# Hybrid decoder block: projection by quarters, the gates' log made in projection, and the experts' gate in one silu

## The reference

```python
hn = rms(x); proj = hn @ w_in              # 1024 -> s5 512 | q 512 | k 512 | v 512 | o 512 | gates 8
y1 = s5_mixer(u)                           # diagonal state space model, glu
q, k = silu(causal_conv(q, k))             # 4 taps
i_pre, f_pre = gates + bias                # 4 heads each
lf = log_sigmoid(f_pre)
y2 = mlstm(q, k, v, i_pre, lf)             # chunks, C, n and m carried; norm; * sigmoid(o)
h = x + concat(y1, y2) @ w_out
t = rms(h); top 4 of 32 experts, softmax gate
# each expert:
h1 = t @ w_up + b_up; g = min(h1[:, :1024], 7); lin = clip(h1[:, 1024:], -7, 7)
y = (g * sigmoid(1.702 * g) * (lin + 1)) @ w_down + b_down
out = rms(h + sum(gate * y))
```

## Time and profile before

| what | us |
|---|---|
| median of 3 runs | 2365.64 (2362.5 to 2370.26) |
| the profiled execution | 2366.74 |
| its span, first to last instruction | 2364.9 |
| project | 0 to 291 |
| mlstm | 294 to 395 |
| s5, output projection and router | 396 to about 655 |
| experts, first to last matmul | 660.5 to 2327 |

### The profile page before, as it was taken

The page is one execution under the profiler, slowest core; times in us unless marked ns, Lnnn a source line. Parts: engine busy times, 40 slices in busy tenths (PEclk is TensorE's granted clock), DMA queues, the critical chain, the costliest instruction groups (busy, mean ns, idle before and its releaser), DMA issues. The chain is left out here.

```text
span 2364.9 us, 32336 instructions
## 1 busy us (share of the span) xinstructions
PE 2166.7 (92%) x10370; PEld 1793.7 (76%) x10371; DVE 1696.4 (72%) x1961; ACT 1214.3 (51%) x1241; POOL 539.6 (23%) x538
## 2 busy tenths in 40 slices
PE   5999866889489999999999999999999999999993
PEld 4787866668368887887888878887887888878772
DVE  4688766646785665778679785887975798677774
ACT  3423143233164554657557664766754576565653
POOL 1001111102520111214124121422411242121411
PEclk9999976999689999999999999999999999999997
DMA  6123271541395666879779885988986798687964
GB/s 174 55 81 134 77 130 36 176 165 54 126 378 204 220 226 190 272 258 325 277 254 375 304 290 209 310 312 275 359 317 191 242 368 311 220 275 257 315 226 178
DMA packets 285814, 540.83 MB, mean 229 GB/s; under 512 B 37155, under 2 KB 53587, under 8 KB 284659
## 3 DMA queue, kind: packets, MB, share of 16 engines
q1 hardware_dynamic: 260306, 490.51, 60.0%
q0 software_dynamic: 25440, 49.47, 8.1%
HBM read 513.06 MB, written 64.57 MB: 244 GB/s over the span
## 5 line engine op out<-in xcount | busy, mean ns | idle before, releaser
L2369 DVE TENSOR_TENSOR ex_w_lo<-ex_raw,ex_w_hi 128x2048 fp32r<-128x2048 f32 x408 | 928.9, 2288 | 264.4 <-ACT ex_w_hi L2263 197.6
L2263 ACT CAST ex_w_hi<-ex_raw 128x2048 fp32r<-128x2048 f32 x371 | 708.2, 1912 | 255.3 <-PE ex_ps_l L2583 80.8
L2174 POOL TENSOR_TENSOR ex_passed<-ex_ident 128x1 f32<-128x1 f32 x136 | 105.2, 774 | 1215.6 <-ACT ex_y L2305 1195.5
L2582 PE MATMUL ex_ps_g<-ex_w_hi,ex_x_hi 128*128 128x512 f32 x784 | 309.2, 394 | 16.3 <-issue 6.4
L2582 PE MATMUL ex_ps_l<-ex_w_hi,ex_x_hi 128*128 128x512 f32 x784 | 308.9, 394 | 1.5 <-DVE ex_w_lo L2369 1.5
L2583 PE MATMUL ex_ps_g<-ex_w_lo,ex_x_hi 128*128 128x512 f32 x784 | 306.6, 391 | 0.0
L2583 PE MATMUL ex_ps_l<-ex_w_lo,ex_x_hi 128*128 128x512 f32 x784 | 305.4, 389 | 0.0
L2582 PE MATMUL ex_ps_y<-ex_w_hi,ex_h_hi 128*128 128x512 f32 x544 | 217.5, 400 | 6.8 <-DVE ex_h_lo L2405 6.8
L2586 PE MATMUL ex_ps_g<-ex_w_hi,ex_x_lo 128*128 128x512 f32 x544 | 212.7, 391 | 0.0
L2586 PE MATMUL ex_ps_l<-ex_w_hi,ex_x_lo 128*128 128x512 f32 x544 | 212.1, 390 | 0.0
L2583 PE MATMUL ex_ps_y<-ex_w_lo,ex_h_hi 128*128 128x512 f32 x544 | 212.0, 390 | 0.0
(11 more groups left out here) (459 smaller groups left out, 3770.9 us busy)
## 6 DMA issues: line engine op xcount, KB each, us to landing
ex_raw<-in_w_up_dram SPq DMA_DIRECT2D x272, 1024.0 KB, 8.2
ex_raw<-in_w_down_dram SPq DMA_DIRECT2D x136, 1024.0 KB, 8.2
st_tab<-tabs SPq DMA_DIRECT2D x8, 1408.0 KB, 7.8
pr_raw<-in_w_in_dram SPq DMA_DIRECT2D x10, 1024.0 KB, 5.5
tabs<-pr_x POOLq DMA_DIRECT2D x32, 256.0 KB, 2.3
por_raw<-in_w_out_dram SPq DMA_DIRECT2D x16, 256.0 KB, 4.4
t<-mix_sig_o SPq DMA_DIRECT2D x8, 512.0 KB, 2.6
fi_h<-h SPq DMA_DIRECT2D x8, 512.0 KB, 7.7
```

Of the source, the lines that this page charges most:

```text
L2174: pool.tensor_tensor(passed[:, :], ident[:, 0:1], ident[:, 0:1], ALU.add).then_inc(passed_done, 1)
L2263: nc.scalar.copy(w_hi[:, j % SPLIT, :, :], raw[:, j % RAW, :, :]).then_inc(hi_done, 1)
L2369: v.tensor_tensor(w_lo[:, j % SPLIT, :, :], raw[:, j % RAW, :, :], w_hi[:, j % SPLIT, :, :].bitcast(F32), ALU.subtract).then_inc(lo_done, 1)
L2582: pe.matmul(to[:, :], hi_in[:, b, kk, :], w_hi[:, s, k, :], start=first, stop=False)
```

## The change

In `project` SP loads tile 3 ahead of piece 1. TensorE turns tiles 0 and 1 and does units 0 to 3 on the first 256 tokens, then on the next 256, into the two halves of the same banks, with the turns of tiles 2 to 7 between. ScalarE and VectorE split piece 0 after tile 1 and piece 1 after tile 2, and put `turned_in` ahead of `square`, and `h_lo` ahead of `mean`. Abs, Exp and Ln of the gates come after the read of unit 40, and VectorE's `min - log` at the end of the block, in place.

In `mlstm` POOL does the memset of `toep` and makes `q_inter` of the next chunk ahead of `power`; VectorE does `gated` ahead of `scales`.

In `experts` ScalarE makes silu(1.702 g) instead of the sigmoid, so VectorE's multiply goes; the limit of the product is 1.702 times as high, and the factor is taken out when `hidden` is copied and split. TensorE does chunks 0 and 1 of the first block, then of the second. The semaphore `sig_done` goes and `glu_done` counts for both; the counts at the other waits are adapted (left out below).

```diff
+        f_abs = raw[0:HEADS, 0, 0:T // PC, :].rearrange("h k n -> h (k n)")
...
-                    if 1 <= j < 1 + PRAW:
-                        load_piece(sp, j - 1)
+                    if j in (1, 3):
+                        load_piece(sp, j // 2)
...
+                    turned_in(j)
+                    if j == 1:
+                        hi(0)
                     if j + 2 < TT:
                         square(j + 2)
-                    turned_in(j)
-                    if j in (1, 2):
-                        hi(j - 1)
+                    if j == 2:
+                        hi(1)
...
+                    if m == LOG_AT:
+                        act.wait_ge(lo_done, len(pieces))
+                        act.wait_ge(unit_read, read_count("gates", 0, 1))
+                        nc.scalar.activation(f_abs, mix["gates"][:, 1, :], ACT.Abs).then_inc(abs_set, 1)
+                        act.wait_ge(abs_set, 1)
+                        nc.scalar.activation(f_abs, f_abs, ACT.Exp, scale=-1.0).then_inc(exp_set, 1)
+                        act.wait_ge(exp_set, 1)
+                        nc.scalar.activation(f_abs, f_abs, ACT.Ln, bias=1.0).then_inc(log_set, 1)
...
-                for j in range(FIRST):
-                    turn(j)
+                turn(0)
+                turn(1)
+                for quarter in range(2):
+
+                    for m in range(FIRST):
+                        n, _, i, _ = units[m]
+                        if m == 0:
+                            pe.wait_ge(t_free, 2 * 2 * (quarter + 1))
+                        if quarter == 0 and i % TILES == 0:
+                            pe.wait_ge(lo_done, n + 1)
+                        cols = slice((i % TILES) * P, (i % TILES + 1) * P)
+                        toks = slice(quarter * 256, (quarter + 1) * 256)
+                        to = acc[m][:, toks]
+                        for k in range(KD):
+                            pe.matmul(to, w_hi[:, n, k, cols], h_hi[:, k, toks], start=(k == 0), stop=False)
+                            pe.matmul(to, w_hi[:, n, k, cols], h_lo[:, k, toks], start=False, stop=False)
+                            mm = pe.matmul(to, w_lo[:, n, k, cols], h_hi[:, k, toks], start=False, stop=(k == KD - 1))
+                        if quarter:
+                            mm.then_inc(unit_ready, 1)
+                            turn(FIRST + m)
+                        elif m < 2:
+                            turn(2 + m)
...
-                    if m < FIRST:
-                        turn(FIRST + m)
...
-                        mean(j + 2)
                     for half in range(2):
                         v.wait_ge(t_hi, 2 * j + half + 1)
                         v.tensor_tensor(h_lo[:, 4 * half:4 * half + 4, j * P:(j + 1) * P],
                                         ps_t[half][:, :].rearrange("p (k t) -> p k t", k=4),
                                         h_hi[:, 4 * half:4 * half + 4, j * P:(j + 1) * P].bitcast(F32),
                                         ALU.subtract).then_inc(t_free, 1)
-                    if j in (1, 2):
-                        lo(j - 1)
+                    if j == 1:
+                        lo(0)
+                    if j + 2 < TT:
+                        mean(j + 2)
+                    if j == 2:
+                        lo(1)
...
+                gate_f = mix["gates"][:, 1, :]
+                v.wait_ge(log_set, 1)
+                v.scalar_tensor_tensor(gate_f, gate_f, 0.0, f_abs, ALU.min, ALU.subtract).then_inc(log_f_set, 1)
+                v.wait_ge(log_f_set, 1)
...
+                pool.memset(st["toep"][:, :, :], 0.0).then_inc(st["zeroed"], 1)
+
+                def query(c):
                     pool.wait_ge(inter_done, c + 1)
                     if c >= 2:
 
                         pool.wait_ge(out_ready, c - 1)
                     pool.tensor_tensor(q_inter[:, c % 2, :, :], q[:, :, steps(c)], w_inter[:, :, :], ALU.mult).then_inc(q_done, 1)
+
+                query(0)
+                for c in range(NC):
+                    if c + 1 < NC:
+                        query(c + 1)
...
-                v.memset(st["toep"][:, :, :], 0.0).then_inc(st["zeroed"], 1)
-                gate_i, gate_f = mix["gates"][:, 0, :], mix["gates"][:, 1, :]
-                v.wait_ge(log_set, 1)
-                link(v.scalar_tensor_tensor(log_f[:, :], gate_f, 0.0, f_abs[:, :], ALU.min, ALU.subtract))
+                gate_i, log_f = mix["gates"][:, 0, :], mix["gates"][:, 1, :]
                 v.wait_ge(consts_set, 11)
-                link(v.tensor_tensor_scan(b[:, :], not_first[:, :], log_f[:, :], 0.0, ALU.mult, ALU.add))
+                link(v.tensor_tensor_scan(b[:, :], not_first[:, :], log_f, 0.0, ALU.mult, ALU.add))
...
+                        gated(c - LAG)
                     if c in NORM_AT:
                         scales(NORM_AT.index(c))
-                    if c >= LAG:
-                        gated(c - LAG)
...
-                        nc.scalar.copy(h_hi[:, b, 4 * half:4 * half + 4, 0:rows],
-                                       ps_t[i % 2][:, :].rearrange("p (k t) -> p k t", k=4)[:, :, 0:rows]).then_inc(
+                        nc.scalar.activation(h_hi[:, b, 4 * half:4 * half + 4, 0:rows],
+                                             ps_t[i % 2][:, :].rearrange("p (k t) -> p k t", k=4)[:, :, 0:rows],
+                                             ACT.Copy, scale=1.0 / ALPHA).then_inc(
...
-                def sigmoid(n, half, blocks, small):
+                def silu(n, half, blocks, small):
                     act.wait_ge(chunk_used, n * CHUNKS + (USED + 4 * half + 2))
                     if half:
                         act.wait_ge(hidden_done, n * 4 + 1)
                     for b in range(blocks):
                         if small and b:
-                            act.wait_ge(glu_done, n * 4 + (2 * half + 1))
+                            act.wait_ge(glu_done, n * 10 + (4 * half + 2))
                         ins = nc.scalar.activation(glu[:, row(half, b, blocks), :], g_bank(half, b, blocks)[:, :],
-                                                   ACT.Sigmoid, scale=ALPHA)
-                    ins.then_inc(sig_done, 1 if small else 2 + 4 * half)
+                                                   ACT.Silu, scale=ALPHA)
+                    ins.then_inc(glu_done, 1 if small else 4 + 2 * half)
...
-                        v.tensor_tensor(h_lo[:, b, rows, :], ps_t[i % 2][:, :].rearrange("p (k t) -> p k t", k=4),
-                                        h_hi[:, b, rows, :].bitcast(F32), ALU.subtract).then_inc(
+                        v.scalar_tensor_tensor(h_lo[:, b, rows, :], ps_t[i % 2][:, :].rearrange("p (k t) -> p k t", k=4), 1.0 / ALPHA,
+                                        h_hi[:, b, rows, :].bitcast(F32), ALU.mult, ALU.subtract).then_inc(
...
-                def gate(n, half, blocks, small):
-                    if small:
-                        fold(n, g_bank(half, 1, blocks), 0, 3 * half + 1).then_inc(glu_done, 1)
-                    v.wait_ge(sig_done, n * 8 + (3 * half + 2))
-                    for b in range(blocks):
-                        at = row(half, b, blocks)
-                        ins = v.tensor_tensor(glu[:, at, :], g_bank(half, b, blocks)[:, :], glu[:, at, :], ALU.mult)
-                    ins.then_inc(glu_done, 1 if small else 2)
+                def gate_fold(n, half, blocks):
+                    fold(n, g_bank(half, 1, blocks), 0, 4 * half + 1).then_inc(glu_done, 1)
...
-                        ins = v.scalar_tensor_tensor(hidden[:, at, :], glu[:, at, :], GLU_MOST, lin[:, at, :], ALU.min, ALU.mult)
+                        ins = v.scalar_tensor_tensor(hidden[:, at, :], glu[:, at, :], ALPHA * GLU_MOST, lin[:, at, :], ALU.min, ALU.mult)
...
-                def multiply(n, kind, j, blocks, full):
+                def multiply(n, kind, j, blocks, full, mine):
...
+                    for b in mine:
...
-                    mm.then_inc(chunk_used, 1)
+                    if mine[-1] == blocks - 1:
+                        mm.then_inc(chunk_used, 1)
 
                 def item(n, kind, blocks, full=None):
-                    for j in range(CHUNKS):
-                        multiply(n, kind, j, blocks, full)
+                    if blocks == 2:
+
+                        for b in range(2):
+                            for j in range(2):
+                                multiply(n, kind, j, blocks, full, (b,))
+                    for j in range(2 * (blocks - 1), CHUNKS):
+                        multiply(n, kind, j, blocks, full, range(blocks))
```

More of the change, by code:

```diff
@@ L2322, in item @@
                         if j in (1, 5):
-                            sigmoid(n, j // 4, blocks, small)
+                            silu(n, j // 4, blocks, small)
                         if j in (6, 8):
@@ L2336, in _ @@
                 act.wait_ge(bias_plus, 1)
-                nc.scalar.activation(warm[0:2 * E, :], bias_rows[0:2 * E, 0:1], ACT.Sigmoid).then_inc(y_a_read, 1)
```

(5 more changed lines are left out.)

43 lines of the change are left out of this document (18 added, 25 removed).

## The result

The changed kernel takes **2332.84 us** (median of 4 runs, 2331.74 to 2334.58), against 2364.07 for the kernel before beside it: the ratio is 0.9864, 95% interval 0.9844 to 0.9885, so it is faster by 31.2 us.

What follows compares the result with a forecast made beforehand. TensorE, busy 92% of the span, was taken as the bound, only its waits recoverable. Projection's start -5, log and mLSTM 0, experts -14.5 made -19.5 on 2364.9; forecast 2346 us, range 2336 to 2353 (8 in 10: 2334 to 2357).

Steps and rivals of the forecast that it cites:

- Projection's start: Projection up to unit 4: first matmul 10.8 us earlier, gain at unit 4 of 5 us, bounds 3 to 8.
- the clock rival: Projection's start: TensorE's clock halves after the new 2.1 us wait, losing 2 to 4 us (2349); no chance given.
- half speed at the start: Projection's first 4.1 us of matmuls run at half speed, costing 2 us before and after alike.
- Gates' log: Projection's end to mLSTM's first scan: log activations cost +1.2 us at projection's end, the scan gains -3.0 (2 to 4).
- mLSTM loop: mLSTM batches: query ahead of power delays the power 0.95 us, `gated` even at the second batch; cost +1.8 (0 to 3).
- The sign named for it: mLSTM's first batch: TensorE's wait for `k_state` would show 0.9 us longer.
- Experts, chunk order: Two-block experts: all four TensorE waits for `x_lo` or `x_hi` covered, -7.9 us (5 to 8.5).
- Experts, silu: Five one-block experts after a small pair: multiplies leave the path to `h_lo`, -6.0 us (0 to 14); `lin` waits stay.
- The half microsecond for refills: Experts: half a microsecond for refills of TensorE's pipe, counted into their total gain.
- its first rival: One-block experts: VectorE is the bound, so the 64 us taken from it come back as time; 2334, chance 0.1.
- the experts' sum of -14.5: Experts' total: chunk order -7.9, silu -6.0 and half a microsecond for refills.

Runs made afterwards that it cites:

- e2: The kernel before with only the gates' logarithm made in the projection and the `toep` memset on GpSimd: 2364.16 us, ratio 0.999.
- e12: The kernel before with only mLSTM's two orders (query ahead of the power, gated output ahead of the scales): 2369.32 us, ratio 0.998.
- e14: The kernel before with only VectorE's gated output put ahead of the scales in mLSTM: 2365.4 us, one run.
- e13: The kernel before with only GpSimd's query put ahead of the power in mLSTM: 2367.56 us, one run.
- e3: The kernel before with only the experts' new chunk order: 2352.5 us, ratio 0.9948.
- e1: The kernel before with only the projection's part (256-token quarters, loads and splits reordered; no log there): 2357.59 us, ratio 0.9965.
- e4: The kernel before with only the experts' silu (no gate multiply on VectorE), old chunk order: 2358.74 us, ratio 0.9972.
- e8: The changed kernel with one-block experts' second transposition of hidden rows issued inside chunk 9, after its first three matmuls: 2324.86 us, ratio 0.9832.
- e7: The changed kernel with 72 idle 128x128 transposes on TensorE ahead of mLSTM's first real one: 2334.21 us.
- e10: e8's kernel with 8 idle 512-column matmuls ahead of mLSTM and three more ahead of the state matmuls of chunks 3 and 5: 2326.53 us, ratio 0.9803.
- e11: The kernel before with 96 idle 4x4 transposes on TensorE at mLSTM's start: 2367.23 us, one run.

## Why the prediction was wrong

- **Projection's start**, -5 forecast, -5.8 measured. All marks held within 0.3 us up to the wait of 2.1 us; the clock rival is real and takes some 2 us in three profiles of nine. On average the term was right. What the prediction calls half speed at the start is the spacing of the matmuls, 0.41 us for 0.227; the granted clock of that row reads 1.00, and the cause of the spacing is open.
- **Gates' log**, +1.2 and -3.0 forecast, +0.3 and -4.05 measured; e2 alone had -3.1 for the second. The activations hide under the last unit's matmuls better than I had them, and GpSimd's constants started 2.8 us behind the last read's end instead of 3.8; why is open. The load shows no drain here either, 282.30 to 283.60.
- **mLSTM loop**, +1.8 forecast. This step failed in its sign: it is -1.8 (79.5 us for 81.3, e12 and e14). I had counted the query's move at its full price and the gated output as "even" at the second batch. In truth the old order already held VectorE for 1 us at each of three batches, which pays for the query's move (e13), and the gated output fills the wait for the power at the second and third batch. The sign named for it did not show either: at the first batch TensorE waited 3.74 us for `k_state`, for 3.79 before, and not 0.9 longer. In the changed kernel S5 still comes 2.6 us late against the scan; the clock there rose 14.3 us behind `a_col`, for 5.5 before.
- **The stretch that the change doesn't touch**, S5 to the experts, 0 forecast, -2.3 measured. The same stretch took 259.8 to 268.0 us over all profiles, 264.2 before and 261.8 after. Nothing shows it to be the change's doing; a span carries it either way.
- **Experts, chunk order**, -7.9 forecast, -11.4 in six of e3's passes: by the starts of matmuls the four waits were 8.5 us and not 7.9, the clock's fall behind one of them 1.6, passes 9 and 15 another 0.7, and 0.6 more went with the four waits.
- **Experts, silu**, -6.0 forecast, -6.5 in five passes and -1.1 in two that I hadn't counted. The `lin` waits stayed, as forecast, and no load of a table came.
- **TensorE's "issue" wait at the end of pass 1**, not in the prediction: -1.8 us.
- **The rest of the experts**, 0 forecast, -1.4: 0.7 in pass 0 and 0.05 or less in most of the others.
- The half microsecond for refills, which the prediction counts as a gain, had the right sign and was small: every wait that goes takes its refill of 0.1 to 0.2 us along, 0.6 for the four waits for x alone.
- One reading of the prediction is uneven: the VectorE work taken away is 98 x 0.69 = 67.6 us, as measured, and not the 64 of its first rival. Nothing hangs on it.

The step that failed is the experts' sum of -14.5, too small by 7.7 us. The chunk order was 3.5 us more than forecast and the silu 1.6: waits were priced by their idle time alone, with hardly anything for what follows them at half clock or in the pipe, and two passes were not counted. The "issue" wait at the end of pass 1, left out of the list, is another 1.8, and the rest of the experts 1.4; against these stands the 0.6 for refills that the sum already had. That the clock fell behind the wait in pass 4 is in part chance: it did so in 6 of 8 profiles. mLSTM's sign comes second. The parts add up: the ratios of e1, e2, e3, e4 and e12 multiply to 0.9856, and the whole is 0.9864 (0.9844 to 0.9885). No gain shows that only the combination has.

## What to carry to other kernels

A short wait of the busiest engine costs more than its idle time: its refill, and behind waits of 2.0 to 2.3 us sometimes a stretch at half clock. Even half-microsecond waits are worth covering, by moving an instruction behind three matmuls (e8, 6.2 us in the experts). Look at what a queue's next instruction shares with the engine that waits, and not only at who waits for whom: two orders of the same operations differed by 1.8 us. And before an unexplained microsecond is put down to an edit, look for "issue" waits beside transfers of the instruction queue, and compare stretches that the edit doesn't touch.

## What the runs showed of the hardware

- The granted clock rose 5.5 to 14.3 us behind the same copy in mLSTM, and the same code did it after 5.5, 5.7 and 11.2 us (before, e4, e3). With TensorE kept busy from 292 it rose at 296.2 (e7). Behind the waits of 2.1 to 2.3 us for `lo(1)` and `x_lo` it fell in 10 of 25 cases, behind the one of 1.7 to 2.2 us at the start of the last pass in 3 of 17 (e2, e4, e10).
- A VectorE multiply of 8 elements in each partition took 1.15 us beside a GpSimd product and 0.17 without (before, e13).
- TensorE stood still for 1.4 to 1.6 us at the end of pass 1 (eight kernels) and for 4.3 us at the experts' start (e7), each ended by nothing that the profile shows and beside a transfer of the instruction queue. 96 idle matmuls more in an earlier stage took the first away (e11), and 72 more on top of the change brought the second (e7).
- Of four chips one gave 2374.6 us for the kernel before, where the others gave 2364.0, 2365.3 and 2365.8. So a time is held against the kernel before on its own chip.
